# Two places of a two-block transformer kernel reordered: the first attention step of the second block inside the last values chunk, and the last gated chunk ahead of two down-projections

## The chip, the cores and the metric

The kernel runs on one NeuronCore of one Trainium2 chip. The metric is the device time of one execution in microseconds, the median of several runs; lower is better. Engines are named as the profile names them: PE (TensorE matmuls) and PEld (its weight loads), ACT (ScalarE), DVE (VectorE), POOL (GpSimd), SP (SyncE, which only issues DMAs here).

## The reference

256 tokens of width 1024 in fp32 pass through two blocks, each of depth 2. Only the parts that the change touches are shown.

```python
def swiglu_ffn(x, w_gu, w_down):                    # first block, FFN_HIDDEN 2816
    gu = x @ w_gu
    g, u = gu[..., :FFN_HIDDEN], gu[..., FFN_HIDDEN:]
    return (jax.nn.silu(g) * u) @ w_down

def conv_ffn(h, w_up, cw, cb, w_down):              # second block, D_FF 2816
    u = dwconv3(h @ w_up, cw) + cb
    g, val = jnp.split(u, 2, axis=-1)
    return (jax.nn.silu(g) * val) @ w_down

def diff_attention(q, k, v, lam):                   # second block, 8 heads
    s = jnp.einsum('bqahd,bkahd->bahqk', q, k).astype(jnp.float32) * (B_QK_DIM ** -0.5)
    p = jax.nn.softmax(s, axis=-1)
    a = (p[:, 0] - lam * p[:, 1]).astype(v.dtype)
    return jnp.einsum('bhqk,bkhe->bqhe', a, v)
```

The second block runs a full layer three times: once for the 256 context tokens (layer 0; keys and values of the context alone, "2 key tiles") and twice for the 256 latent tokens (layers 0 and 1; keys and values of latents and context, "4 key tiles"). Each of the three has one `diff_attention` and one `conv_ffn`.

## The kernel before

**Weights as a stream.** Every weight matrix is cut on the host into 908 units of 128 x 1024 fp32 (512 KB), in the order in which they are used. SP loads them into four slots `raw`. ACT converts a unit to the high part (`whi`, `hi_part`, L1017), POOL subtracts to get the low part (`wlo`, L448), and PE multiplies three times, high x high, high x low and low x high (L469 to L471 with features as the output's partitions, L495 to L497 with tokens). A unit of the usual kind is 24 matmuls of 256 columns, a unit of a token chunk 12 of 512 columns. `hi_part` for a unit waits until PE has finished the unit four places earlier (`units_used`), so ACT and POOL are at most four units ahead of PE, and everything that ACT does in between stands in the same queue as these conversions.

**The feed-forward.** `ffn_units` gives the order: 11 chunks `gate_up(j)` of four units and 11 `down_pair(j)` of two. Chunk 0 first, then for i = 0 to 4: gate_up(2i+1), down_pair(2i), gate_up(2i+2), down_pair(2i+1); the last pair, for chunk 10, is cut in halves (`last_blocks`). Between a chunk and its pair, `hidden` turns the chunk in PSUM `lin` into the operand of the pair. With the convolution (second block) that is: DVE 12 operations on 128 x 256 (L1827, L1830, L1834), ACT Silu (L1263), DVE product (a `tt_`, L1458), ACT copy to the high part `br_hi` (L1265), DVE subtraction to `br_lo` (L1458), which raises `hid_lo`, for which PE waits before the pair. ACT stands in `hidden` from the chunk's end until `br_hi` is written, and makes its next conversion only then. The operand tiles have two buffers, by the parity of the chunk. In the first block there is no convolution, and the chain is short.

**The second block's attention.** `second_layer` ends its projections with two token chunks (`token_chunk(0)`, `token_chunk(1)`: the values of heads 0 to 3 and 4 to 7). ACT copies each out of PSUM (L1034) and then raises `values_ready`. Then PE runs 16 steps n (8 heads x 2 query tiles): `diff_scores(n)` (L909), DVE `highest` (maximum of both halves L1992, then a small product with the query scale, L1458), ACT `diff_exps` (L1319, which first needs the Exp table), DVE `combine` (reciprocal L2001, small product L1458, L2004, L2006), PE `diff_transposes` (L916), ACT `transposed` (L1070), PE `diff_values` (L925). Units of the following gate and branch projections are put between them (`advance(fill, ...)`): one before the transposes, one or two before the values. Scores of n+1 are issued right after the transposes of n, those of n = 0 ahead of everything, after a wait for `qk_done` and `values_ready`. On ACT, the Exp of the two lambdas (L1376; it loads the Exp table) and `diff_exps(0)` stand behind the copy of the last values chunk; DVE waits for `lam_exp` before `highest(0)`. The order is written out by hand on every engine, and the engines meet only by semaphores.

Of the kernel before, what the change touches and what calls it, by code (L numbers as in the profile page):

```python
# [11 lines left out]
P, D, T, L = 128, 1024, 256, 2  # L12
KD = D // P
CH = 512
SLOTS, UNIT = 4, 1024
FFN = 2816
NCH = FFN // 256
# [50 lines left out]
def ffn_units(chunk, unit, gu, down):  # L68
    def gate_up(j):
        chunk(gu, j * CH)  # L70

    def down_pair(j):
        for k in (2 * j, 2 * j + 1):
            unit(down, [(k, 0)], D)

    gate_up(0)
    for i in range(NCH // 2):
        gate_up(2 * i + 1)
        down_pair(2 * i)
        gate_up(2 * i + 2)  # L80
        down_pair(2 * i + 1)
    for half in range(2):
        unit(down, [(2 * NCH - 2, half * CH), (2 * NCH - 1, half * CH)], CH)
# [127 lines left out]
def build(nc, a, n_units, n_first, n_dve):  # L211
    with ExitStack() as ctx:
# [238 lines left out]
        def _(pe):  # L451
# [121 lines left out]
            def ffn(after=(), context_norm=False):  # L573
# [13 lines left out]
                for b in range(4):  # L587
                    pe.matmul(aux[:, b, :].rearrange("p (n t) -> p n t", n=8),
                              zero_w[:, 0:1].to_broadcast([P, P]), zero_w[:, :].unsqueeze(1).to_broadcast([P, 8, 64]), start=True, stop=False, skip_group_check=True)
                for _ in range(NCH // 2):  # L590
                    feature_chunk(1)
                    down(0)
                    feature_chunk(0)
                    down(1)
                pe.wait_ge(hid_lo, t.next(hid_lo))
                for h in range(2):
                    last_blocks(aux_tile, 0, h, (br_hi, br_lo))

# [320 lines left out]
            def diff_values(n, kts):  # L919
                h, tt = divmod(n, 2)  # L920
                if tt == 0 and t.ahead(yb_taken, 0):
                    pe.wait_ge(yb_taken, t.ahead(yb_taken, 0))
                pe.wait_ge(pt_ready, t.next(pt_ready))
                for kt in range(kts):
                    mm = pe.matmul(aux[:, 3, tt * P:(tt + 1) * P], probs_tr[:, kt * P:(kt + 1) * P], head_values(h, kt, kts),  # L925
                                   start=(kt == 0), stop=(kt == kts - 1))
                mm.then_inc(pv_done, 1)
                if tt == 1:
                    t.skip(yb_taken)
# [19 lines left out]

            def second_layer(kts, rotate, start):  # L950
                start()
                token_chunk(1)
                feature_chunk(0, after={2: spatial_mix})
                for c in range(4):
# [5 lines left out]
                    else:  # L960
                        token_chunk(0, after=after)
                token_chunk(1)
                pe.wait_ge(qk_done, t.ahead(qk_done, 0))
                pe.wait_ge(values_ready, t.next(values_ready))
                fill = second_fill()
                diff_scores(0, kts)
                for n in range(STEPS):
# [33 lines left out]
            token_chunk(1, after={0: lambda: spread_inverse(0)})  # L1001
            second_layer(4, True, lambda: feature_chunk(0, fresh=QUARTERS))
            second_layer(4, True, normed_chunk)

        @block.scalar
        def _(act):
# [246 lines left out]
            def ffn(conv, context_norm=False):  # L1253
                def hidden(p, units):
                    hi_parts(units)
# [8 lines left out]
                    act.wait_ge(hid_f32, t.next(hid_f32))  # L1264
                    act.activation(br_hi[:, p * CH:(p + 1) * CH], zt(base + 12 + 2 * p, 2), ACT.Copy).then_inc(hid_hi, 1)  # L1265

                hidden(0, 4)
                for i in range(NCH // 2):
                    hidden(1, 4)
                    hidden(0, 6)  # L1270
                    if context_norm and i == NCH // 2 - 1:
                        for q in range(4):
                            quarter_hi(q, ctx_scaled[:, quarter(q)])
                    hi_parts(2)


# [68 lines left out]
            def second_layer(l, x, kts, rotate, normed=None):  # L1345
# [23 lines left out]
                values_chunk(0, zt(v, 4), qk_roots)  # L1369
                values_chunk(1, zt(v + 4, 4))  # L1370
                act.drain()
                if rotate and l == 1:
                    act.wait_ge(kv_landed, t.next(kv_landed, 32))
                act.drain().then_inc(values_ready, 1)
                act.wait_ge(lam_sum, t.next(lam_sum))
                act.activation(small[:, 18:20], small[:, 16:18], ACT.Exp).then_inc(lam_exp, 1)  # L1376
                fill = second_fill()
                diff_exps(0, kts)
                for n in range(STEPS):
# [69 lines left out]
        def _(dve):  # L1449
# [369 lines left out]
            def ffn(l, conv, context_norm=False):  # L1819
                def hidden(p, count, j):  # L1820
                    if conv:
# [26 lines left out]
                    else:  # L1848
                        settle().then_inc(lin_free[p], 1)
                    dve.wait_ge(hid_hi, t.next(hid_hi))  # L1850
                    tt_(br_lo[:, p * CH:(p + 1) * CH], h, br_hi[:, p * CH:(p + 1) * CH].bitcast(F32),
                        ALU.subtract).then_inc(hid_lo, 1)

                hidden(0, 4, 0)
                for i in range(NCH // 2):
                    hidden(1, 4, i * 2 + 1)
                    hidden(0, 6, i * 2 + 2)
                    lo_parts(2)
                    if context_norm and i < 4:
                        context_quarter(i)  # L1860
                if context_norm:
                    for q in range(4):
                        quarter_lo(q, ctx_scaled[:, quarter(q)])
# [407 lines left out]
```

## Time and profile before

| | |
|---|---|
| median of 3 runs | 3052.51 us (3045.93 to 3053.8) |
| the profiled execution | 3043.33 us |
| its span, first to last instruction | 3041.5 us |
| mean granted TensorE clock | 0.972 |
| PE, ACT, DVE, POOL busy | 96%, 50%, 36%, 72% |
| DMA | 495 MB, 163 GB/s |

The profile is of one execution, which was 9.2 us faster than the median of the three timed ones. A timeline row gives start, length, engine, line, operation, what it writes and reads, its shape, and in brackets the idle time of the engine before it and what ended it. "PEclk" is the clock that the throttle granted, 1.00 being 2.4 GHz and 0.50 being 1.2 GHz.

### The profile page before, as it was taken

Reading aid. Unit: us, or ns where it says so; the run is one execution under the profiler, and the core shown is the slowest. Engines: PE = TensorE matmul, PEld = TensorE weight load, DVE = VectorE, ACT = ScalarE, POOL = GpSimd, SP = SyncE. Lnnn points to the kernel's source line nnn. Section 1 sums busy time; section 2 is a strip of 40 time slices with the busy share of each in tenths; the row PEclk is TensorE's granted clock in tenths of the full one; section 3 lists DMA queues with packets and bytes.
Section 4 is the critical chain, followed back from the end, with each engine's and each line's share of the span. In section 5 each row is a group of like instructions: output and inputs, shape, how many; then the busy total and the mean of one; then the engine's idle time right before and its main releaser. Section 6 shows DMA issues by size and latency. Waiting matters only on the chain.

```text
span 3041.5 us, 51872 instructions
## 1 busy us (share of the span) xinstructions
PE 2924.7 (96%) x21822; PEld 2695.1 (89%) x21822; DVE 1080.1 (36%) x1976; ACT 1516.7 (50%) x1999; POOL 2177.2 (72%) x912
## 2 busy tenths in 40 slices
PE   7998989999999999999999999999999999899998
PEld 7887969989878879989899999878899989789998
DVE  2412412023214232221563433426624343464433
ACT  4666464455665454453564444445544444465443
POOL 6667687886667678886576886665576866557686
PEclk9999999999999989999999999999999999999999
DMA  6445455554445455554344554543354554334454
GB/s 219 140 152 179 148 191 176 182 196 164 152 151 183 164 176 180 186 196 148 132 152 153 179 177 151 189 133 118 126 173 146 187 175 154 124 125 160 152 177 150
DMA packets 136521, 495.39 MB, mean 163 GB/s; under 512 B 15072, under 2 KB 17760, under 8 KB 135136
## 3 DMA queue, kind: packets, MB, share of 16 engines
q1 hardware_dynamic: 131904, 480.53, 47.3%
q10 hardware_dynamic: 4384, 11.54, 1.1%
q8 instruction: 172, 2.82, 0.4%
q14 instruction: 61, 0.50, 0.1%
HBM read 488.86 MB, written 3.15 MB: 162 GB/s over the span
## 4 chain that ended last, share of the span: by engine, by line
PE 83%; ACT 5%; DVE 5%; DVEq 2%; POOL 2%; issue 1%; ACTq 1%; DMA 1%; SPq 0%
PE lin L469 18%; PE lin L470 17%; PE lin L471 17%; PE aux L469 4%; PE aux L471 4%; PE aux L470 4%; PE lin L495 2%; PE lin L496 2%; PE lin L497 2%; PE aux L562 2%; ACT whi L1017 2%; POOL wlo L448 2%; PE aux L909 1%; PE aux L633 1%; PE aux L925 1%
## 5 line engine op out<-in xcount | busy, mean ns | idle before, releaser
L448 POOL TENSOR_TENSOR wlo<-raw,whi 128x1024 fp32r<-128x1024 f32 x908 | 2177.0, 2414 | 850.0 <-ACT whi L1017 849.3
L1017 ACT ACTIVATE whi<-raw 128x1024 fp32r<-128x1024 f32 x908 | 949.7, 1057 | 990.3 <-PE lin L471 731.9
L469 PE MATMUL lin<-in_hi,whi 128*128 128x256 f32 x3968 | 1148.7, 289 | 24.7 <-POOL wlo L448 22.0
L470 PE MATMUL lin<-in_lo,whi 128*128 128x256 f32 x3968 | 1130.2, 285 | 0.0
L471 PE MATMUL lin<-in_hi,wlo 128*128 128x256 f32 x3968 | 1129.6, 285 | 0.0
L469 PEld LDWEIGHTS lin<-in_hi,whi 128*128 128x128 f32 x3968 | 769.2, 194 | 62.6 <-issue 52.7
L470 PEld LDWEIGHTS lin<-in_lo,whi 128*128 128x128 f32 x3968 | 769.6, 194 | 0.6
L471 PEld LDWEIGHTS lin<-in_hi,wlo 128*128 128x128 f32 x3968 | 768.7, 194 | 0.0
L469 PE MATMUL aux<-br_hi,whi 128*128 128x256 f32 x880 | 250.0, 284 | 7.6 <-DVE br_lo L1458 7.6
L471 PE MATMUL aux<-br_hi,wlo 128*128 128x256 f32 x880 | 249.8, 284 | 0.0
L470 PE MATMUL aux<-br_lo,whi 128*128 128x256 f32 x880 | 249.7, 284 | 0.0
L469 PE MATMUL lin<-br_hi,whi 128*128 128x256 f32 x768 | 224.6, 292 | 0.0
L470 PE MATMUL lin<-br_lo,whi 128*128 128x256 f32 x768 | 220.4, 287 | 0.0
L471 PE MATMUL lin<-br_hi,wlo 128*128 128x256 f32 x768 | 220.3, 287 | 0.0
L469 PEld LDWEIGHTS aux<-br_hi,whi 128*128 128x128 f32 x880 | 169.7, 193 | 8.2 <-DVE br_lo L1458 8.2
L471 PEld LDWEIGHTS aux<-br_hi,wlo 128*128 128x128 f32 x880 | 169.7, 193 | 0.0
L470 PEld LDWEIGHTS aux<-br_lo,whi 128*128 128x128 f32 x880 | 169.6, 193 | 0.0
L1827 DVE TENSOR_SCALAR Z<-lin,par_all 128x256 f32<-128x256 f32 x132 | 62.7, 537 | 272.7 <-PE lin L471 272.7
L469 PEld LDWEIGHTS lin<-br_hi,whi 128*128 128x128 f32 x768 | 150.5, 196 | 5.3 <-issue 3.5
L470 PEld LDWEIGHTS lin<-br_lo,whi 128*128 128x128 f32 x768 | 150.5, 196 | 0.2
L471 PEld LDWEIGHTS lin<-br_hi,wlo 128*128 128x128 f32 x768 | 150.5, 196 | 0.0
L1458 DVE TENSOR_TENSOR Z<-Z,lin 128x512 f32<-128x512 f32 (+1 forms) x34 | 29.8, 876 | 306.3 <-ACT Z L1263 277.1
(247 smaller groups left out, 3663.4 us busy)
## 6 DMA issues: line engine op xcount, KB each, us to landing
raw<-in_wstream SPq DMA_DIRECT2D x908, 512.0 KB, 3.3
Z<-in_rel ACTq DMA_DIRECT2D x2, 1536.0 KB, 7.3
Z<-in_mem_t ACTq DMA_DIRECT2D x2, 1024.0 KB, 7.4
kv_store<-Z ACTq DMA_DIRECT2D x2, 1024.0 KB, 6.9
Z<-kv_store ACTq DMA_DIRECT2D x2, 1024.0 KB, 10.8
x<-in_x_t SPq DMA_DIRECT2D x1, 1024.0 KB, 4.8
Z<-in_ctx_t SPq DMA_DIRECT2D x1, 1024.0 KB, 4.8
out_x<-x SPq DMA_DIRECT2D x1, 1024.0 KB, 3.8
```

What stands on the lines that cost most here:

```text
L448: pool.tensor_tensor(wlo[s][:, :], raw[s][:, :], whi[s][:, :].bitcast(F32), ALU.subtract).then_inc(lo_pool, 1)
L469: pe.matmul(out, wh, xh, start=start, stop=False, skip_group_check=True)
L470: pe.matmul(out, wh, xl, start=False, stop=False, skip_group_check=True)
L471: return pe.matmul(out, wl, xh, start=False, stop=stop, skip_group_check=True)
L495: pe.matmul(out, xh, wh, start=start, stop=False, skip_group_check=True)
L496: pe.matmul(out, xh, wl, start=False, stop=False, skip_group_check=True)
L497: return pe.matmul(out, xl, wh, start=False, stop=stop, skip_group_check=True)
L562: mm = pe.matmul(square_sums(b)[:, tt:tt + 1], zt(tiles + k)[:, tt * P:(tt + 1) * P], ones[:, 0:1], start=(k == 0 and tt == 0), stop=(k == ...
L633: mm = pe.matmul(out, q[:, tt * P:(tt + 1) * P], k[:, 0:(tt + 1) * P], start=True, stop=True)
L909: mm = pe.matmul(aux[:, m, 0:kts * P], q, head_keys(m, h, kts), start=True, stop=True)
L1017: act.activation(whi[s][:, :], raw[s][:, :], ACT.Copy).then_inc(hi_ready, 1)
L1827: dve.tensor_scalar(o[c], u[c], w[c][:, 1:2], w[c][:, 3:4], ALU.mult, ALU.add)
```

## The change

1. In each of the five feed-forwards, the last two chunks stand together: ... down_pair(7), gate_up(9), gate_up(10), down_pair(8), down_pair(9), and the halves for chunk 10. For that the operand tiles have three buffers (chunk modulo 3). ACT's conversions and, where it is there, its work on the context norm are divided anew over the end of the feed-forward. No unit is added or dropped.
2. In each of the three second layers, PE issues `diff_scores(0)` after the second of the four units of the last values chunk, behind a wait for `qk_done` and, in the last layer, for `kv_landed` (the loads of the stored context keys and values). `values_ready` is now waited for ahead of the first `diff_values`. On ACT the two-lambda Exp comes before the last values chunk's conversions, three conversions follow, then `diff_exps(0)`, then the fourth conversion and the copy. DVE and POOL keep their order.

```diff
@@ ffn_units
-    for i in range(NCH // 2):
+    for i in range(NCH // 2 - 1):
         gate_up(2 * i + 1)
         down_pair(2 * i)
         gate_up(2 * i + 2)
         down_pair(2 * i + 1)
+    for j in (NCH - 2, NCH - 1):
+        gate_up(j)
+    for j in (NCH - 3, NCH - 2):
+        down_pair(j)
@@ PE, ffn
-                for _ in range(NCH // 2):
+                for i in range(NCH // 2 - 1):
                     feature_chunk(1)
-                    down(0)
+                    down(2 * i % 3)
                     feature_chunk(0)
-                    down(1)
+                    down((2 * i + 1) % 3)
+                feature_chunk(1)
+                feature_chunk(0)
+                down((NCH - 3) % 3)
+                down((NCH - 2) % 3)
                 pe.wait_ge(hid_lo, t.next(hid_lo))
                 for h in range(2):
-                    last_blocks(aux_tile, 0, h, (br_hi, br_lo))
+                    last_blocks(aux_tile, (NCH - 1) % 3 * 2, h, (br_hi, br_lo))
@@ PE, diff_values
+                if n == 0:
+                    pe.wait_ge(values_ready, t.next(values_ready))
@@ PE, second_layer
+                def first_scores():
+                    pe.wait_ge(qk_done, t.ahead(qk_done, 0))
+                    if stored:
+                        pe.wait_ge(kv_landed, t.next(kv_landed, 32))
+                    diff_scores(0, kts)
...
-                token_chunk(1)
-                pe.wait_ge(qk_done, t.ahead(qk_done, 0))
-                pe.wait_ge(values_ready, t.next(values_ready))
+                token_chunk(1, after={1: first_scores})
                 fill = second_fill()
-                diff_scores(0, kts)
@@ ACT, ffn (DVE's hidden alike: buffer j % 3)
-                for i in range(NCH // 2):
-                    hidden(1, 4)
-                    hidden(0, 6)
-                    if context_norm and i == NCH // 2 - 1:
-                        for q in range(4):
-                            quarter_hi(q, ctx_scaled[:, quarter(q)])
+                for i in range(NCH // 2 - 1):
+                    hidden(2 * i + 1, 4)
+                    hidden(2 * i + 2, 6)
                     hi_parts(2)
+                hidden(NCH - 2, 4)
+                hidden(NCH - 1, 4)
+                for q in range(4):
+                    if context_norm:
+                        quarter_hi(q, ctx_scaled[:, quarter(q)])
+                    hi_part()
@@ ACT, second_layer
                 values_chunk(0, zt(v, 4), qk_roots)
-                values_chunk(1, zt(v + 4, 4))
+                act.wait_ge(lam_sum, t.next(lam_sum))
+                act.activation(small[:, 18:20], small[:, 16:18], ACT.Exp).then_inc(lam_exp, 1)
+                hi_parts(3)
+                diff_exps(0, kts)
+                evacuate(1, 1, zt(v + 4, 4))
                 act.drain()
                 if rotate and l == 1:
                     act.wait_ge(kv_landed, t.next(kv_landed, 32))
                 act.drain().then_inc(values_ready, 1)
-                act.wait_ge(lam_sum, t.next(lam_sum))
-                act.activation(small[:, 18:20], small[:, 16:18], ACT.Exp).then_inc(lam_exp, 1)
                 fill = second_fill()
-                diff_exps(0, kts)
```

## Rows read from the trace of the kernel before

**Rows 1.** The page's first part, busy time and share of the span by engine.

```profile
PE 2924.7 (96%) x21822; PEld 2695.1 (89%) x21822; DVE 1080.1 (36%) x1976; ACT 1516.7 (50%) x1999; POOL 2177.2 (72%) x912
```

**Rows 2.** PE's waits: us in total, how often, longest.

```profile
PE aux L916 <- DVE probs L2006: 19.1, 11, 3.2
PE aux L469 <- DVE br_lo L1458: 7.6, 3, 2.5
PE aux L909 <- ACTq L1374: 6.9, 3, 2.3
```

**Rows 3.** Timeline of PE at the three attention starts.

```profile
1452.64 0.44 PE L916 MATMUL aux<-c,probs 128*128 128x128 f32 x2 [0.32 <-DVE probs L2006]
...
2050.23 1.12 PE L916 MATMUL aux<-c,probs 128*128 128x128 f32 x4 [2.89 <-DVE probs L2006]
...
2607.07 1.13 PE L909 MATMUL aux<-Z 64*128 64x512 f32 x4 [2.30 <-ACTq L1374]
...
2614.47 0.66 PE L916 MATMUL aux<-c,probs 128*128 128x128 f32 x4 [3.22 <-DVE probs L2006]
```

**Rows 4.** Timeline of ACT at the third attention start.

```profile
2594.95 1.01 ACT L1034 ACTIVATE Z<-lin 128x1024 f32<-128x1024 f32 x1
...
2602.14 1.06 ACT L1017 ACTIVATE whi<-raw 128x1024 fp32r<-128x1024 f32 x1 [1.66 <-PE lin L497]
2604.86 1.06 ACT L1017 ACTIVATE whi<-raw 128x1024 fp32r<-128x1024 f32 x1 [1.66 <-PE lin L497]
...
2606.99 1.28 ACT L1376 ACT_TABLE_LOAD   x1 [0.15 <-issue]
...
2610.51 0.75 ACT L1319 ACTIVATE aux<-aux,small,qk_inv 128x512 f32<-128x512 f32 x1 [2.03 <-DVEq L1995]
```

**Rows 5.** Timeline of DVE at the same place.

```profile
2608.52 0.16 DVE L1458 TENSOR_TENSOR small<-small 128x1 f32<-128x1 f32 x1 [19.02 <-ACT small L1376]
...
2608.99 1.23 DVE L1992 TENSOR_REDUCE small<-aux 128x2 f32<-128x1024 f32 x1
...
2612.19 0.17 DVE L2001 RECIPROCAL small<-small 128x2 f32<-128x2 f32 x1 [1.74 <-ACTq L1320]
...
2613.67 0.75 DVE L2006 SCALAR_TENSOR_TENSOR probs<-aux,small,probs 128x512 f32<-128x512 f32 x1
```

**Rows 6.** A small DVE product beside POOL: timelines, and its group.

```profile
1461.33 2.40 POOL L448 TENSOR_TENSOR wlo<-raw,whi 128x1024 fp32r<-128x1024 f32 x1 [0.41 <-ACT whi L1017]
...
1461.76 1.98 DVE L1458 TENSOR_TENSOR small<-small,qk_inv 128x2 f32<-128x2 f32 x1
...
L1458 DVE TENSOR_TENSOR small<-small,qk_inv 128x2 f32<-128x2 f32 x48 | 38.0, 791 | 3.6
```

**Rows 7.** Timelines of PE, ACT and DVE at the second convolution feed-forward's end.

```profile
2472.45 0.39 PE L469 MATMUL aux<-br_hi,whi 128*128 128x256 f32 x1 [2.52 <-DVE br_lo L1458]
...
2469.66 0.63 ACT L1263 ACTIVATE Z<-Z 128x512 f32<-128x512 f32 x1 [4.32 <-DVEq L1837]
...
2471.58 1.99 ACT L1017 ACTIVATE whi<-raw 128x1024 fp32r<-128x1024 f32 x2
...
2470.32 0.69 DVE L1458 TENSOR_TENSOR Z<-Z 128x512 f32<-128x512 f32 x1 [0.74 <-ACT Z L1263]
...
2471.70 0.69 DVE L1458 TENSOR_TENSOR br_lo<-Z,br_hi 128x512 fp32r<-128x512 f32 x1 [0.69 <-ACT br_hi L1265]
```

**Rows 8.** Timeline of POOL over that feed-forward's last two chunks.

```profile
2455.43 9.50 POOL L448 TENSOR_TENSOR wlo<-raw,whi 128x1024 fp32r<-128x1024 f32 x4 [3.06 <-ACT whi L1017]
...
2462.52 7.13 POOL L448 TENSOR_TENSOR wlo<-raw,whi 128x1024 fp32r<-128x1024 f32 x3
```

**Rows 9.** Stretches: length, busy (instructions) of PE, PEld, DVE, ACT, POOL, PEclk, DMA.

```profile
1447.00:1455.00 8.00, 7.61 (x45) 6.53 (x46) 3.54 (x10) 4.00 (x8) 2.82 (x2) 0.79 0.33 126
2047.00:2059.00 12.00, 9.11 (x48) 7.08 (x48) 4.86 (x10) 5.57 (x11) 2.35 (x1) 0.72 0.13 47
...
2860.00:3020.00 160.00, 160.00 (x1336) 160.00 (x1335) 60.74 (x128) 69.18 (x77) 130.10 (x55) 1.00 0.54 180
```

More of the change, by code:

```diff
@@ L948, in branch_transposes, with second_layer @@
                         mm.then_inc(yb_trans, 1)
-            def second_layer(kts, rotate, start):
+            def second_layer(kts, rotate, start, stored=False):
+                def first_scores():
[3 more added lines that the diff above has]
+                    diff_scores(0, kts)
                 start()
@@ L1001, in _ @@
             token_chunk(1, after={0: lambda: spread_inverse(0)})
-            second_layer(4, True, lambda: feature_chunk(0, fresh=QUARTERS))
-            second_layer(4, True, normed_chunk)
+            for l in range(L):
+                second_layer(4, True, normed_chunk if l else lambda: feature_chunk(0, fresh=QUARTERS), l == 1)
         @block.scalar
@@ L1253, in ffn, with hidden @@
             def ffn(conv, context_norm=False):
-                def hidden(p, units):
+                def hidden(j, units):
+                    p, b = j % 2, j % 3
                     hi_parts(units)
@@ L1264, in hidden @@
                     act.wait_ge(hid_f32, t.next(hid_f32))
-                    act.activation(br_hi[:, p * CH:(p + 1) * CH], zt(base + 12 + 2 * p, 2), ACT.Copy).then_inc(hid_hi, 1)
+                    act.activation(br_hi[:, b * CH:(b + 1) * CH], zt(base + 12 + 2 * p, 2), ACT.Copy).then_inc(hid_hi, 1)
                 hidden(0, 4)
-                for i in range(NCH // 2):
-                    hidden(1, 4)
-                    hidden(0, 6)
-                    if context_norm and i == NCH // 2 - 1:
-                        for q in range(4):
-                            quarter_hi(q, ctx_scaled[:, quarter(q)])
-                    hi_parts(2)
+                for i in range(NCH // 2 - 1):
+                    hidden(2 * i + 1, 4)
+                    hidden(2 * i + 2, 6)
+                    hi_parts(2)
+                hidden(NCH - 2, 4)
[4 more added lines that the diff above has]
+                    hi_part()
             def rms(x, fresh=False, then=None):
@@ L1819, in ffn, with hidden @@
             def ffn(l, conv, context_norm=False):
-                def hidden(p, count, j):
+                def hidden(j, count):
+                    p, b = j % 2, j % 3
                     if conv:
@@ L1850, in hidden @@
                     dve.wait_ge(hid_hi, t.next(hid_hi))
-                    tt_(br_lo[:, p * CH:(p + 1) * CH], h, br_hi[:, p * CH:(p + 1) * CH].bitcast(F32),
+                    tt_(br_lo[:, b * CH:(b + 1) * CH], h, br_hi[:, b * CH:(b + 1) * CH].bitcast(F32),
                         ALU.subtract).then_inc(hid_lo, 1)
[L1854 to L1857, printed above, removed]
+                hidden(0, 4)
+                for i in range(NCH // 2 - 1):
+                    hidden(2 * i + 1, 4)
+                    hidden(2 * i + 2, 6)
                     lo_parts(2)
-                    if context_norm and i < 4:
+                    if context_norm:
                         context_quarter(i)
+                hidden(NCH - 2, 4)
+                hidden(NCH - 1, 4)
+                lo_parts(4)
                 if context_norm:
```

## Prediction

> **What bounds the kernel now.** First the page's busy times: PE works 96% of the span, POOL 72% [rows 1]. Then a stretch in the middle of a feed-forward: 1336 matmuls in 160 us without a pause, at full clock [rows 9]. That is 0.120 us each, so a unit of 24 matmuls takes 2.87 us, two 5.75, four 11.5. No reordering makes that shorter. A change of order can win only where PE stands still, and what the clock loses there. So the third view is the list of PE's waits [rows 2]. Three of its groups lie where the diff moves something: DVE's `br_lo` before a feed-forward's last halves (7.6 us, 3 times, always in the convolution form), ACT at L1374, which is `values_ready`, before the first scores (6.9 us, 3 times), and DVE's `probs` before transposes (19.1 us, 11 times). Of these 11, three are the first step of an attention, 0.32, 2.89 and 3.22 us [rows 3], in sum 6.43; the other eight (12.7 us) belong to later steps, which the change leaves as they are. The two feed-forwards without convolution wait nowhere at that point, so reordering them gives nothing.
>
> **Part 1, the feed-forward's end.** Count from G, the end of the last gate-up chunk. In the second convolution feed-forward PE's wait ends at 2472.45 after 2.52 us [rows 7], and two units stand before it, so G = 2472.45 - 2.52 - 5.75 = 2464.18. The chain that starts there has Silu at G+5.5, DVE's product at G+6.1, ACT's next conversions at G+7.4 and `br_lo` ready at G+8.2 [rows 7]. It needs 8.2 us and has two units of cover. After the change four units stand there, 11.5 us, a margin of 3.3. Chunk 9 has chunk 10 and pair 8 as cover, 17.2 us. The gap goes three times: 7.6 us.
>
> What is late next? ACT makes no conversion while it is in that chain, and now two chains follow each other after four units, not six. After chunk 9 the first conversion starts at G9+7.4, and POOL's product from 8.5 to 11.0 (in the trace 2455.43, G9 being 2446.9 [rows 8]). PE wants that unit at 11.5: margin 0.5, the same as in every turn of the old loop. POOL then has four units back to back, 9.50 us [rows 8], until G9+18.05, which is G10+6.5. DVE's product of chunk 10 reads two SBUF tiles and starts at G10+6.1. Such a product waits for POOL: a 128 x 2 one took 1.98 us and ended with POOL's instruction of 1461.33 to 1463.73 [rows 6]. So it loses at most 0.4 us, the conversion starts by G10+7.8, POOL is done at 7.8+1.06+0.08+2.40 = 11.35, and PE wants the unit at 11.5. I take 0; the bounds are 0 and a whole POOL instruction less the margin, 2.4-0.5 = 1.9 each, 5.7 in all. The third buffer costs no instruction. The halves' units come in the same number and size, and SP's queue only sees another order.
>
> **Part 2, the first attention step.** Take the third start and count from A, the end of the second unit of the last values chunk. The scores now start at 2607.07 after a wait of 2.30, so the chunk ends at 2604.77 [rows 3]. Conversions released by its units start 2.72 apart [rows 4], so a unit is 2.72 and A = 2599.33. After the change:
> - PE: scores 0 to 1.1 (1.13 [rows 3]), third unit to 3.8, fourth to 6.5, then the first fill unit. That takes 3.05 (from 2608.20, the scores' end, to 2611.25, where the wait of 3.22 begins [rows 3]), until 9.55. Then PE wants the transposes.
> - ACT: the first values copy ends at A-3.4 [rows 4]; table load 1.28 and the Exp follow, to about -1.75, beside PE's first two units. The first conversion starts at -1.7 instead of -2.6 and has 8 us in hand. The second starts at 0.1. The third waits for the third unit: 3.9 to 4.95. Only then come the exponentials, 1.68 us (2610.51 to DVE's reciprocal at 2612.19 [rows 4, 5]), to 6.6. The fourth conversion waits for the end of the fourth unit (6.5) anyway and loses 0.1. So does the values copy behind it, which ends near 8.7; the new wait for `values_ready` stands before `diff_values(0)` at about 14.3 (9.55, transposes 0.66, scores 1.13, a unit 3.05) and costs nothing.
> - DVE: it now stood idle 19.02 us for the lambda Exp [rows 5]; afterwards that is long done. Maximum from 1.2 to 2.45. The small product meets POOL, whose instruction for the second conversion runs until about 4.25, and waits for it, but the exponentials start at 4.95 in any case. After them the reciprocal at 6.65, then a small product that meets POOL's third instruction (5.0 to 7.4), then L2004 and L2006, some 1.7 of the 2.23 us from reciprocal to the end of L2006 [rows 5]: probabilities at 9.1 to 9.3 against 9.55.
>
> Both waits go: 6.9 + 6.43 = 13.3 us. The first start has 2 key tiles, shorter operations and more margin. `kv_landed` in the last layer is for loads that ACT issues at the layer's start, ten chunks earlier, and costs 0; if late it would have held `values_ready` too. What is late next is the second small product: if it misses the gap between two POOL instructions it waits to 10.1, probabilities come at 11.8, and PE waits 2.2 us, in two starts 4.4. That is the bound.
>
> This meeting is where a rule of the Trainium skill speaks against the change: SBUF — State Buffer, "Who interferes with whom", calls the port pair of VectorE and GpSimd an exclusive lock, so that a VectorE instruction with two SBUF inputs is blocked for the whole of a GpSimd one. The trace agrees (1.98 us for two columns [rows 6]). By that rule alone the old place had a merit, POOL being idle there; by the times above the lock is mostly covered.
>
> **The clock.** Around two of the three attention starts the granted clock was low, 0.79 over 8 us and 0.72 over 12 us [rows 9]; a third stretch, 8 us around the wait of 2472.45 [rows 7], repeats the row with 0.79. At half clock PE loses 8 x 0.21 + 12 x 0.28 + 8 x 0.21 = 6.7 us, some 0.7 of it while it waited. All three follow a wait that goes; the other three places had such waits at full clock. I take 6.0, with 0 and 10 (all six places) as bounds. TensorE: Matmul & The Clock Gate, "What's actually happening", says that the monitor's window runs free and that a kernel's slow matmuls differ in number from run to run; no run here shows it for one place.
>
> **The sum.** 7.6 + 13.3 + 6.0 = 26.9 us. Against the profiled execution's 3043.3 that is 3016.4. But that execution was 9.2 us below the median of the timed runs, 3052.5, and I forecast a median: 3052.5 - 26.9 = **3025.6, say 3026**.
>
> **Rivals.**
> - *The clock part doesn't come*, because slow stretches fall elsewhere. For it: three of six such waits had none. Gain 20.9: 3031.6. Chance 0.15.
> - *POOL's lock gives half of it back*: 2.2 us in two starts and 1.9 us at three feed-forwards' ends, 10.1 in all. For it: margins of 0.2 to 0.5 us. Against it: every term is from rows of the same code at other places. 3035.7; with the slow clock back after the new waits 3041.7. Chance 0.12. The Trainium skill's lock rule, named above, gives this case if the lock falls badly every time.
> - *The scores don't start the chain earlier* (part 2 does not do what it says), since ACT's queue order, not PE, holds the probabilities. Against it: the exponentials end at 6.6 by the rows. Only part 1 with its clock share is left, 7.6 + 1.7: 3043.2. Chance 0.06.
> - *Slower*: the earlier first step shifts DVE against POOL in all 48 steps, so that each small product with `qk_inv` waits a whole POOL instruction, 2.40, and not the mean of 0.79 [rows 6]. That adds 1.61 to each step's chain, 77 us if nothing covers it: 3103. It decides from 0.56 us a step (26.9 / 48). For it: eight later steps already wait for `probs`, so the cover is thin. Against it: each step starts anew at its transposes, and the order inside the loop is the same. Chance 0.05.
>
> **How the numbers follow.** The forecast has 0.62, with a range of its own of 3015 to 3035 (clock part 0 to 10, some microseconds between sessions). With the first two rivals it makes 0.89; a range of 3013 to 3041 leaves out the last two and the tails. A measurement of this kernel can tell about 0.3%, 9 us, from no change. Faster by more, below 3043.4: 0.62 + 0.15 + 0.12 less tails, 0.87. Within: 0.08, of which the third rival is most. Slower: 0.05.
>
> **What would show it.** In the profile after, L909's first scores stand between L495 to L497 matmuls with no idle time before them; the first L916 of each attention has no idle time of 0.3 us or more; `br_lo` no longer appears among PE's waits with 2.5 us, and no `wlo` wait stands before the last halves. The eight later waits stay near 12.7 us in sum. I am wrong if new `wlo` waits appear at the feed-forwards' ends, if the first L916 waits 2 us, or if the later `probs` waits grow.

## The result and the profile after

The changed kernel takes 3018.61 us (median of 4 runs) against 3051.14 us for the kernel before, measured on the same chip; the ratio is 0.9899, 95% interval 0.9882 to 0.9917, which is 25 to 36 us less. A second measurement gave 3023.53 against 3046.28, ratio 0.9921 (0.9901 to 0.9941), 18 to 30 us less. The forecast was 3026, that is 26.9 us less than the 3052.5 it started from.

The page's first part of the changed kernel, and three rows of PE's waits (us in total, how often, longest):

```profile
PE 2919.8 (97%) x21822; PEld 2692.0 (89%) x21822; DVE 1097.9 (36%) x1976; ACT 1515.8 (50%) x1999; POOL 2179.8 (72%) x912
...
PE aux L924 <- DVE probs L2028: 12.6, 8, 2.9
PE aux L566 <- ACT Z L1301: 4.8, 5, 3.5
PE aux L473 <- POOL wlo L452: 1.8, 2, 0.9
```

Of the three groups of [rows 2], `probs` has gone from 19.1 us in 11 waits to 12.6 in 8. `br_lo` before the last halves and `values_ready` before the first scores appear no more, and no `wlo` wait has taken their place (1.8 us in 2 waits, as before). The second row has grown: the token sums of a norm wait 4.8 us for ACT's squares, where they waited 3.4 (L562 in the kernel before).

The third attention start, to be laid beside [rows 3 to 5]. PE (matmul rows of the scores and the transposes), ACT, DVE, then POOL:

```profile
2583.52 1.13 PE L917 MATMUL aux<-Z 64*128 64x512 f32 x4
...
2593.05 0.49 PE L924 MATMUL aux<-c,probs 128*128 128x128 f32 x3
...
2580.24 1.28 ACT L1388 ACT_TABLE_LOAD   x1
...
2587.71 1.06 ACT L1030 ACTIVATE whi<-raw 128x1024 fp32r<-128x1024 f32 x1 [2.96 <-PE lin L501]
2588.68 0.73 ACT L1336 ACTIVATE aux<-aux,small,qk_inv 128x512 f32<-128x512 f32 x1
...
2584.70 1.23 DVE L2014 TENSOR_REDUCE small<-aux 128x2 f32<-128x1024 f32 x1 [2.53 <-PE aux L917]
2586.00 1.53 DVE L1476 TENSOR_TENSOR small<-small,qk_inv 128x2 f32<-128x2 f32 x1
2590.34 0.17 DVE L2023 RECIPROCAL small<-small 128x2 f32<-128x2 f32 x1 [2.81 <-ACTq L1337]
2590.58 0.68 DVE L1476 TENSOR_TENSOR small<-small 128x1 f32<-128x1 f32 x1
...
2592.00 0.75 DVE L2028 SCALAR_TENSOR_TENSOR probs<-aux,small,probs 128x512 f32<-128x512 f32 x1
...
2582.77 4.75 POOL L452 TENSOR_TENSOR wlo<-raw,whi 128x1024 fp32r<-128x1024 f32 x2 [0.98 <-ACT whi L1030]
2588.85 2.40 POOL L452 TENSOR_TENSOR wlo<-raw,whi 128x1024 fp32r<-128x1024 f32 x1 [1.33 <-ACT whi L1030]
```

Neither PE row has idle time in brackets: both waits are gone. With A = 2583.52 the probabilities are ready at 2592.75, A+9.2, and PE turns to the transposes at A+9.5. Both small products end with a POOL instruction: the first takes 1.53 us until 2587.53 (POOL's pair ends at 2587.52), the second 0.68 until 2591.26 (POOL ends at 2591.25).

The end of the second convolution feed-forward, against [rows 7 and 8], and the start of the last layer behind it. The first two rows are the kernel before at that start (ACT's last conversion ahead of the norm, and PE's token sums), all others the changed kernel:

```profile
2477.17 1.06 ACT L1017 ACTIVATE whi<-raw 128x1024 fp32r<-128x1024 f32 x1 [3.60 <-PE aux L471]
2482.20 1.15 PE L562 MATMUL aux<-c,Z 128*128 128x1 f32 x8 [2.25 <-ACT Z L1284]
...
2452.03 2.94 ACT L1030 ACTIVATE whi<-raw 128x1024 fp32r<-128x1024 f32 x3
...
2450.55 0.91 DVE L1476 TENSOR_TENSOR Z<-Z 128x512 f32<-128x512 f32 x1 [0.75 <-ACT Z L1277]
2452.16 0.69 DVE L1476 TENSOR_TENSOR br_lo<-Z,br_hi 128x512 fp32r<-128x512 f32 x1 [0.70 <-ACT br_hi L1279]
...
2453.15 11.81 POOL L452 TENSOR_TENSOR wlo<-raw,whi 128x1024 fp32r<-128x1024 f32 x5 [2.24 <-ACT whi L1030]
...
2455.59 0.33 SPq L441 DMA_DIRECT2D raw<-in_wstream  x1
...
2460.11 1.06 ACT L1030 ACTIVATE whi<-raw 128x1024 fp32r<-128x1024 f32 x1 [3.03 <-DMA raw<-in_wstream]
2460.12 0.34 ACTq L1363 DMA_DIRECT2D Z<-in_sgu_w  x1
...
2463.17 1.28 ACT L1295 ACT_TABLE_LOAD   x1 [2.00 <-issue]
...
2462.73 2.27 DVE L1473 TENSOR_SCALAR mod<-mods_all 128x48 f32<-128x48 f32 x1
...
2455.76 0.30 PE L473 MATMUL aux<-br_hi,whi 128*128 128x256 f32 x1
2465.15 0.37 PE L566 MATMUL aux<-c,Z 128*128 128x1 f32 x1 [3.45 <-ACT Z L1301]
```

`br_lo` is ready at 2452.85, 2.9 us before PE starts the last halves at 2455.76. POOL, which ACT's chain held idle for 2.24 us, then runs five instructions back to back until 2464.96, past the end of the feed-forward (2461.70, where PE's wait of 3.45 us begins). A slot of the weight stream comes free only when POOL has read it, so SP issues the transfer of the unit that ACT converts at 2460.11 only at 2455.59, when the first of the five is done, and ACT waits 3.03 us for it to land. ACT's load issues, its table load and the first square (2464.47) follow in its queue, and PE's token sums wait 3.45 us, where they waited 2.25.

**A way to count.** In every kernel of this study PE's time can be split into three parts. I take the second part of the execution, from the wait of 0.52 us in the token sums near 1330 us to PE's last product. Ahead of it the change takes no wait away (PE's idle time there is 65.5 and 69.3 us in the two executions of before, 65.6 and 65.9 in the two of the changed kernel), yet over all traces it began between 1323.0 and 1331.8 us. Within the second part I add up PE's idle times over 0.3 us, and half of the time at granted clock 0.50. What is left is called PE's own work (where PE waited at half clock, half of that time is counted twice, and the rest comes out smaller by it):

| kernel | second part | idle | clock | rest | timed ratio to before (95%) |
|---|---|---|---|---|---|
| before | 1708.1 | 43.0 | 37.5 | 1627.6 | |
| before_again | 1703.9 | 42.2 | 34.1 | 1627.6 | |
| after | 1681.9 | 24.1 | 30.7 | 1627.1 | 0.9899 (0.9882 to 0.9917) |
| after_again | 1683.0 | 24.1 | 32.4 | 1626.5 | 0.9921 (0.9901 to 0.9941) |
| attn_only | 1690.9 | 29.6 | 34.1 | 1627.2 | 0.9932 (0.9911 to 0.9953) |
| ffn_only | 1696.3 | 35.7 | 32.4 | 1628.2 | 0.9961 (0.9944 to 0.9977) |
| busy_before | 1703.6 | 24.7 | 30.7 | 1648.2 | 0.9984 (0.9970 to 0.9998) |
| scores_u3 | 1684.0 | 25.9 | 30.7 | 1627.4 | 0.9905 (0.9875 to 0.9934) |
| double_small | 1683.7 | 26.5 | 27.3 | 1629.9 | 0.9925 (0.9896 to 0.9953) |
| late_loads | 1682.1 | 22.6 | 30.7 | 1628.8 | 0.9918 (0.9898 to 0.9938) |
| square_psum | 1673.1 | 16.7 | 29.0 | 1627.4 | 0.9877 (0.9857 to 0.9898) |
| both_fix | 1674.6 | 18.6 | 27.3 | 1628.7 | 0.9884 (0.9866 to 0.9902) |
| all_fix | 1668.5 | 18.6 | 22.2 | 1627.7 | 0.9876 (0.9858 to 0.9895) |
| before_square | 1691.3 | 34.7 | 27.3 | 1629.3 | 0.9952 (0.9933 to 0.9970) |

The rest agrees within 3.4 us over all kernels but the one that adds products. So the means of two executions each say where the gain is: 23.6 us (1706.0 to 1682.4), of which 18.5 is idle time (42.6 to 24.1) and 4.2 clock (35.8 to 31.6). The clock alone moves by 1.7 and 3.4 us between the two executions of one kernel, as much as the 4.2 us, so the clock's share of the gain isn't secured by this table. Over the whole span the two executions of each differ by 22.0 us (3041.5 and 3040.0 against 3017.7 and 3019.8).

### The profile page after: what moved, and what is told of

Read it like the earlier page. It is cut to its first block, busy times and chain, and to the rows that moved or that the text cites. A ratio compares the mean times of both kernels' runs of the same rounds, so it can differ in the third digit from the quotient of the medians.

```text
span 3017.7 us, 51871 instructions
## 1 busy us (share of the span) xinstructions
PE 2919.8 (97%) x21822; PEld 2692.0 (89%) x21822; DVE 1097.9 (36%) x1976; ACT 1515.8 (50%) x1999; POOL 2179.8 (72%) x912
## 4 chain that ended last, share of the span: by engine, by line
PE 83%; ACT 5%; DVE 4%; POOL 2%; DVEq 2%; issue 1%; ACTq 1%; DMA 1%; SPq 0%
PE lin L473 18%; PE lin L474 17%; PE lin L475 17%; PE aux L473 4%; PE aux L475 4%; PE aux L474 4%; POOL wlo L452 2%; PE lin L499 2%; PE aux L566 2%; PE lin L501 2%; PE lin L500 2%; ACT whi L1030 2%; PE aux L641 1%; PE aux L917 1%; PE lin L616 1%
## 6 DMA issues: line engine op xcount, KB each, us to landing
Z<-kv_store ACTq DMA_DIRECT2D x2, 1024.0 KB, 12.7
```

## The experiments

### The two halves of the change

attn_only is the kernel before with the attention hunks of the diff, ffn_only the one with the feed-forward hunks; after_again is the changed kernel once more, on the same chip.

> The changed kernel once more, on the chip on which its two halves are timed. By the sum of the prediction, 7.6 + 13.3 us of waits and about 6 us of clock, it stands 27 us under the kernel before; the first measurement had 25 to 36 us. Theory A: what the two parts gain alone adds up to this gain, to within 3 us. Theory B: the gain has a third source, over 26.9 us, that comes only with both; then the sum of the parts falls short by 5 us or more.

> Only the first attention step is moved; the feed-forwards are those of before. Theory A: the three waits before the first scores (6.9 us) and the three before the first transposes (6.4 us) go, with 0 to 5 us of clock: 13 to 18 us faster than before, some 3035. PE still waits 2.52 us three times for br_lo. Rival, POOL's lock catches the second small product: 4.4 us of that come back as probs waits, 9 to 14 us faster.

> Only the feed-forward's order and its third buffer; the attention's start is that of before. Theory A: three waits of 2.52 us go, 7.6 us, with 0 to 3 us of clock, less about 1.4 us at the last block's start, where in the changed kernel the token sums waited 3.45 us and not 2.25: 6 to 9 us faster, some 3043. Rival, the two chains close together hold POOL up and PE waits for wlo before the last halves: 0 to 4 us faster, with new wlo waits of 1 us or more.

Measured: 0.9932 is 21 us less (14 to 27) for the attention, 0.9961 is 12 us less (7 to 17) for the feed-forward. By the second part they are 15.1 and 9.7 us, in sum 24.8, against 23.6 with both. The parts add up to within 1.2 us, and theory A holds; a third source would have left 5 us. PE's idle time says the same: 13.0 us less for the attention (13.3 forecast), 6.9 for the feed-forward (7.6 forecast). The timed medians can't decide it: their parts make 33 us against 24 with both, with intervals of 5 to 7 us to each side of every figure. The waits split cleanly. PE's waits in attn_only, then in ffn_only:

```profile
PE aux L916 <- DVE probs L2012: 12.6, 8, 2.9
PE aux L469 <- DVE br_lo L1464: 7.6, 3, 2.5
...
PE aux L924 <- DVE probs L2022: 19.3, 11, 2.9
PE aux L917 <- ACTq L1386: 6.9, 3, 2.3
PE aux L566 <- ACT Z L1296: 3.1, 5, 2.0
```

attn_only keeps the three `br_lo` waits and has lost the first-step ones; ffn_only is the reverse. The wait of the token sums, which I had put down to the reorder with 1.4 us, was 2.0 us in ffn_only, no longer than before. The traces of all kernels show why. Let E be the end of the second feed-forward. ACT's last conversion before the sums can start at E-2.78, when PE frees its slot. In the old order its transfer was issued at E-11.2 to E-12.7 and had 8 us and more to land. In the new order it is issued at E-6.1 in all nine traces, which leaves 3.3 us. In two of them (ffn_only, double_small) it landed within that, in the other seven it took 4.3 to 5.0 us, and the conversion came 0.9 to 1.7 us late. So it is the reorder that takes the room away, and the transfer's time in the execution at hand that decides whether the conversion is late. A second part of the wait doesn't depend on it: from this conversion to the table load ACT's five load issues took 2.5 to 3.2 us, but 3.75 in double_small, which waited 2.96 us though its transfer had landed in time.

### The clock alone

```diff
                 pe.wait_ge(qk_done, t.ahead(qk_done, 0))
+                keep_busy(10)
                 pe.wait_ge(values_ready, t.next(values_ready))
...
                     advance(fill, DIFF_BEFORE_T[n])
+                    if n == 0 and kts == 4:
+                        keep_busy(12, 3)
                     diff_transposes(n, kts)
...
+                if second:
+                    pe.wait_ge(lin_free[1], t.ahead(lin_free[1]))
+                    for _ in range(11):
+                        pe.matmul(lin[:, 1, 0:CH]...)
                 pe.wait_ge(hid_lo, t.next(hid_lo))
```

> The kernel before with its order untouched; PE fills most of the waits that the change removes with products nobody reads: 10 before the wait for values_ready (three places), 12 before the first transposes (the two starts with four key tiles), 11 before the wait for br_lo (three places), about 0.21 us each at full clock. The output is that of before. No wait is shortened, so this shows the clock's share alone. Theory A, the half-clock stretches around these places follow from PE's standing still: 3 to 8 us faster than before, and the three stretches at the third and fourth of these places gone. Theory B, they fall where they fall: no difference, or up to 3 us slower where a product runs past the end of its wait.

> The kernel before once more, for where its half-clock stretches fall. Theory A, they follow the waits: of the nine waits that the change removes (2.3 to 3.2 us each, one of 0.3 to 1.8) again some three are followed by such a stretch within 8 us, and the second part's clock loss is 34 to 38 us. Theory B, chance: they fall at other places, and as often where PE does not wait.

Measured: 0.9984, 5 us less, with the interval from 1 to 9; by the second part 2.4 us less than the mean of the two executions of before, with 5.1 us less clock loss and 2 to 3 us lost where a product ran past the end of its wait or a wait was not quite filled. The timed gain lies in theory A's range of 3 to 8 us, the trace's 2.4 us just under it. The granted clock (last but two columns: PEclk) around such a wait, in attn_only and in ffn_only where it stays, and in busy_before where the waits of 2035 to 2055 and of 2455 to 2470 are filled:

```profile
2458.00:2470.00 12.00, 9.48 (x67) 9.28 (x66) 6.36 (x14) 4.22 (x5) 8.44 (x5) 0.86 0.53 172
...
2590.00:2606.00 16.00, 11.79 (x64) 8.41 (x63) 4.91 (x10) 8.01 (x12) 7.78 (x4) 0.89 0.40 129
...
2035.00:2055.00 20.00, 19.61 (x125) 14.23 (x124) 6.56 (x14) 10.03 (x16) 9.71 (x5) 1.00 0.35 112
2455.00:2470.00 15.00, 14.87 (x115) 13.28 (x115) 9.22 (x20) 5.28 (x6) 11.96 (x6) 1.00 0.57 181
```

Counting places over all traces says more. The change touches six places (three attention starts, three feed-forward ends). In the executions that still wait 2.3 us or more there (before, before_again, before_square, and the kept half of attn_only and ffn_only) these are 24 places, and in 14 of them PE's clock fell to half from about the wait's end; which ones differed between two executions of the same kernel (3 of 6 each time, two of them the same). Where the wait is gone or filled there are 60 places, and in none did it fall (one of these, the first attention start of busy_before, still waited 1.9 us). So the fall follows PE's standing still, and which of the waits is hit changes from one execution to the next, as theory A of before_again had it (its clock loss, 34.1 us, lies in the forecast range). The half-clock stretches at the six places cost 6.8 us in before, 5.1 in before_again and 6.8 in before_square. In the total this hardly shows, since the stretches at other places differ as much: before_square, which has these waits, lost 27.3 us, less than either trace of the changed kernel (30.7 and 32.4). The Trainium skill, TensorE: Matmul & The Clock Gate, "What's actually happening", says the monitor runs free of the kernel; the traces agree, with 14 of 24.

### How much room the first step has

```diff
-                token_chunk(1, after={1: first_scores})
+                token_chunk(1, after={2: first_scores})
```

> The changed kernel with the first scores one unit (2.72 us) later, behind the third unit of the last values chunk and not the second. By the prediction's chain: maximum A+3.9 to 5.2, the small product waits for POOL's instruction of A+5.0 to 7.4, exponentials to 9.3, probabilities at A+11.9 against a need at 9.55. Theory A: PE waits about 2.4 us for probs in the two starts with four key tiles and 0.5 to 1.5 in the first, 5 to 6 us slower than the changed kernel in all. Theory B, the chain has more room than worked out: no such waits, no difference.

Measured: the second part is 1.6 us longer than the changed kernel's mean; `probs` waits come back at the two starts with four key tiles, but of 0.45 and 0.78 us, not 2.4. That is neither theory A (5 to 6 us slower) nor B (no waits). PE, DVE and POOL at the third start:

```profile
2589.65 0.55 PE L924 MATMUL aux<-c,probs 128*128 128x128 f32 x3 [0.78 <-DVE probs L2028]
...
2584.39 1.24 DVE L1476 TENSOR_TENSOR small<-small,qk_inv 128x2 f32<-128x2 f32 x1
...
2587.61 0.16 DVE L1476 TENSOR_TENSOR small<-small 128x1 f32<-128x1 f32 x1
...
2578.44 7.17 POOL L452 TENSOR_TENSOR wlo<-raw,whi 128x1024 fp32r<-128x1024 f32 x3 [0.97 <-ACT whi L1030]
2588.61 2.36 POOL L452 TENSOR_TENSOR wlo<-raw,whi 128x1024 fp32r<-128x1024 f32 x1 [3.00 <-ACT whi L1030]
```

The scores come 2.72 us later and the probabilities only some 1.1 us later against PE's need (0.3 us ahead of it before, 0.78 behind now). My sum let POOL's instructions stand where they were. But POOL works on what ACT converts, and ACT's exponentials now stand ahead of the fourth conversion: POOL runs dry for 3.00 us, and just then the second small product finds it idle and takes 0.16 us. The chain that is late makes room for itself. The placement in the change has 0.3 us to spare (A+9.2 against A+9.5); one unit later it misses by 0.45 and 0.78 us.

### The slower rival

```diff
+                    tt_(small[:, 224:226], stat(n, "minus"), query_scale(n), ALU.mult)
+                    settle()
                     tt_(stat(n, "minus"), stat(n, "minus"), query_scale(n), ALU.mult)
```

> The changed kernel with the small product with qk_inv (128 x 2, two SBUF inputs, 0.16 us when free, mean 0.79) done twice in each of the 48 steps, the first time into scratch. It prices the rival in which DVE and POOL meet badly in every step. Theory A, the steps' chains are covered but for the eight that already wait: 0.3 to 2.4 us in each of these, 2 to 19 us slower than the changed kernel. Theory B, nothing covers the steps: 48 times 0.8 us and more, 38 us slower or worse.

Measured: 0.9925, and a second part 1.3 us longer than the changed kernel's mean. PE's waits for `probs`, which were 12.6 us in 8 waits:

```profile
PE aux L924 <- DVE probs L2030: 15.4, 10, 3.4
```

2.8 us more in sum. The clock loss is 4.3 us smaller than the changed kernel's mean in this execution; without it the second part is 5.5 us longer, 2.4 of them idle. Theory A (2 to 19 us), near its lower end: the steps have cover, also against a product that meets POOL, and the waits that exist grow by 0.2 to 0.8 us. The first product of a pair takes the wait for POOL, the second is then free (median of all 96 is 0.163 us).

### What makes the later steps wait

The eight waits that the change leaves are the largest thing left in the attention. Before one of them, DVE's square of a head's output stands in the queue ahead of the next maximum. DVE and POOL of the changed kernel before the wait of 2.87 us at 2637.72:

```profile
2630.34 0.41 DVE L2034 TENSOR_SCALAR probs<-aux 128x256 f32<-128x256 f32 x1
2630.88 2.43 DVE L2036 SCALAR_TENSOR_TENSOR probs<-probs 128x256 f32<-128x256 f32 x1
...
2630.63 2.39 POOL L452 TENSOR_TENSOR wlo<-raw,whi 128x1024 fp32r<-128x1024 f32 x1 [0.53 <-ACT whi L1030]
```

The square has both inputs in SBUF and ends 0.3 us after POOL's instruction; the clamp ahead of it reads PSUM and takes its 0.41 us beside the same POOL instruction. So the square is given one input from PSUM, at the price of one more clamp, of the head's output in PSUM:

```diff
                     dve.tensor_scalar(sq, y, 2.0 ** 64, -2.0 ** 64, ALU.min, ALU.max)
-                    settle().then_inc(yb_taken, 1)
-                    dve.scalar_tensor_tensor(sq, sq, 2.0 ** -10, sq, ALU.mult, ALU.mult)
+                    dve.tensor_scalar(y, y, 2.0 ** 64, -2.0 ** 64, ALU.min, ALU.max)
                     settle()
+                    dve.scalar_tensor_tensor(sq, y, 2.0 ** -10, sq, ALU.mult, ALU.mult)
+                    settle().then_inc(yb_taken, 1)
```

> The changed kernel, where DVE's squares of the head outputs (24, one for every two steps, two SBUF inputs, 0.42 us when free, median 1.84, up to 2.6) take one input from PSUM, at the price of one more clamp of 0.42 us each. The output stays. Theory A, the eight waits for probs in later steps (12.6 us) come from this square waiting for POOL: they fall to about 4 us (2.9 to 1.4, 2.6 to 1.1, the short ones to 0), 8 to 11 us faster than the changed kernel. Theory B, ACT's or PE's order sets them: the squares get short and the waits stay.

> The kernel before, with nothing but the squares of the head outputs taking one input from PSUM. Theory A, the eight later waits for probs come from the squares in the old order too: the group falls from 19.1 us to about 12 (the three first steps, 6.4, and 5.2), some 9 us faster than before; the waits that the change removes stay. Theory B, without the change's earlier first step the waits of later steps are set otherwise and stay near 12.7 us.

Measured: square_psum is at 0.9877 of before, its second part 9.3 us shorter than the changed kernel's. The groups of the squares (count | busy, mean ns) in the changed kernel and in square_psum, the waits for `probs` in square_psum and in before_square:

```profile
L2036 DVE SCALAR_TENSOR_TENSOR probs<-probs 128x256 f32<-128x256 f32 x24 | 37.4, 1557 | 3.0
...
L2037 DVE SCALAR_TENSOR_TENSOR probs<-aux,probs 128x256 f32<-128x256 f32 x24 | 10.2, 424 | 2.0
...
PE aux L924 <- DVE probs L2028: 5.2, 6, 1.2
...
PE aux L916 <- DVE probs L2006: 9.9, 9, 2.9
PE aux L469 <- DVE br_lo L1458: 7.6, 3, 2.5
PE aux L909 <- ACTq L1374: 6.9, 3, 2.3
```

24 squares go from 1557 to 424 ns. The waits fall by 7.4 us after the change, and by 9.2 us in the old order (19.1 to 9.9, where about 12 was expected; one first step waits 1.4 us there and not 2.9, behind a stretch at half clock). before_square's second part is 14.7 us shorter than before's mean where some 9 us was forecast; 7.9 of them are idle time, and 8.5 are clock, which its edit can't be credited with from one execution. Theory A in both: the three waits of 2.6 to 2.9 us shrink to 1.0 to 1.2, the two of 1.2 go, and only the two of 0.8 us stay as they were and have another cause.

### The start of the last layer

late_loads moves ACT's five load issues of the last layer behind the token norm; both_fix adds the edit of square_psum; all_fix also loads the norm's table ahead of the feed-forward's last conversion.

```diff
+                if normed is not None:
+                    rms(x, normed, ACT.Gelu_apprx_tanh)
                 act.dma_start(zt(S2, 2), a["sgu_w"]...)
...
-                if normed is not None:
-                    rms(x, normed, ACT.Gelu_apprx_tanh)
```

> The changed kernel, with ACT's five loads at the last block's start issued behind the token norm and not ahead of it (in the other two blocks that start without a norm nothing changes). In the changed kernel the token sums there waited 3.45 and 3.8 us for ACT's square, behind a conversion whose transfer landed late (2460.11), 3.0 us of issues and a table load of 1.28. Theory A, the issues stand on the path: the wait is 1.2 to 1.8 us, some 2 us faster than the changed kernel, 26 to 30 us faster than before by the sum of waits. Theory B, the late transfer alone sets it: the wait stays at 3 us or more and the time is that of the changed kernel.

> The changed kernel with the squares of the head outputs taking one input from PSUM and with ACT's loads behind the token norm. Theory A, the two are independent: 9.4 us (second part of square_psum against that of the changed kernel, by its trace) and 0 to 2 us for the loads, 9 to 11 us faster than the changed kernel, 33 to 36 us faster than before. Theory B, with the waits for probs gone POOL and ACT fall differently and the loads' gain turns negative: not faster than square_psum by its trace.

> both_fix, and ACT loads the table for the token norm ahead of the feed-forward's last conversion, where it stands idle for 2 to 3 us, and not behind it. Theory A, the table load of 1.28 us stands on the path to the token sums: the wait there falls from 1.5 to 0.3 us, those of 0.4 to 0.5 us at the other start go, 1.5 us faster than both_fix by the trace. Theory B, the residual or the late transfer holds the sums: the wait stays above 1 us.

Measured: in late_loads the wait falls to 1.49 us, as theory A said, but the idle time in all falls by 1.5 us only, since new waits appear, and the second part is no shorter (1682.1 against 1682.4), the rest being 2.1 us larger, which is inside the scatter of 3.4 us. Two new waits of PE in late_loads, the same two in both_fix, and what DVE did in both_fix:

```profile
2489.57 0.47 PE L499 MATMUL lin<-whi,in_hi 128*128 128x512 f32 x1 [0.70 <-POOL wlo L452]
2509.96 1.27 PE L909 MATMUL aux<-Z 128*128 128x128 f32 x9 [0.59 <-DVE Z L2076]
...
2477.73 0.47 PE L499 MATMUL lin<-whi,in_hi 128*128 128x512 f32 x1 [0.91 <-POOL wlo L452]
2500.03 1.16 PE L909 MATMUL aux<-Z 128*128 128x128 f32 x8 [2.54 <-DVE Z L2077]
...
2477.46 0.29 DVE L1476 TENSOR_TENSOR probs<-Z 128x128 f32<-128x128 f32 x1 [5.21 <-DMA Z<-in_lam]
2477.67 2.35 DVE L1476 TENSOR_TENSOR small<-par_all,c 128x1 f32<-128x1 f32 x1
...
2494.78 5.20 DVE L2077 TENSOR_SCALAR Z<-Z,small 128x512 f32<-128x512 f32 x2
```

The issues take their 3 us of ACT's queue wherever they stand: now they hold up the conversions behind the norm, and DVE waits 5.21 us for the lambdas to land. DVE's two `TENSOR_SCALAR` then fall beside POOL and take 5.20 us, where the changed kernel's took 1.33 at the same place. In late_loads theory A was right on the wait, and its 2 us of gain don't show; in both_fix theory B holds, 1.9 us more idle time than square_psum and a second part 1.5 us longer. all_fix cuts the wait to 0.56 us, but at the other start a wait of 2.04 us appears for DVE (1850.87), and its idle time is that of both_fix, 18.6 us. Its shorter second part is clock (22.2 against 27.3 us), which one execution can't credit to the edit. all_fix (3009.49, ratio 0.9876) and square_psum (3011.69, 0.9877) can't be told apart; both are faster than the changed kernel by their ratios to before (0.9899 and 0.9921) and by the trace.

## Why the prediction was right

- **What bounds the kernel, and the gap sum.** 6.9 + 6.43 + 7.6 = 20.9 us of waits were to go, and all nine went. PE's idle time fell by 18.5 us only. The missing 2.4 us are waits that grew elsewhere: 1.5 us in the mean are the token sums at the last layer's start (2.25 and 2.09 before, 3.45 and 3.83 after), 0.4 the same sums one layer earlier, the rest smaller ones.
- **Part 1.** Right in each number that could be read: chunk 10's product lost 0.22 us to POOL (0.91 instead of 0.69; at most 0.4 forecast), POOL stood idle 2.24 us and was done with the halves' unit 0.2 us before PE wanted it (0.15 forecast). The failed step is "The halves' units come in the same number and size, and SP's queue only sees another order". The number is the same, but they reach POOL in one block of five instructions, a slot comes free later, and the transfer behind it has 3.3 us to land, not 8 or more. I followed POOL to the last halves and not to the end of the stream that it feeds.
- **Part 2.** First conversion, exponentials, maximum, both meetings with POOL and the probabilities at A+9.2 came within 0.35 us of the forecast. The bound of 2.2 us a start, POOL's lock falling badly, was too dark: the runs give 0.5 us for the second small product, and scores_u3 shows why it can't fall much worse, since POOL runs dry when ACT is in the exponentials.
- **The clock.** Forecast 6.0 with 0 and 10 as bounds; 4.2 by two pairs of traces, and filling the waits alone gave 5 us (1 to 9) timed and 5.1 us less clock loss. Both traced figures are differences of a size that one kernel's executions show among themselves; that 6.0 was so near is in part luck. At the places themselves before lost 6.8 and 5.1 us in its two executions. The reason given, that slow stretches follow these waits and not others, is what 14 of 24 against 0 of 60 shows. That "all three follow a wait that goes" was right, but which three was chance, and part of it came back: in both traces of the changed kernel a stretch of 13.7 us at half clock stands at the longer wait of the token sums, where it was 10.2 us in both of before.
- **The rivals.** Clock part absent: excluded by busy_before only just (interval 1 to 9 us), by the count of places clearly. POOL's lock gives 10.1 us back: not so, no `wlo` or first-step `probs` wait is there. Scores don't start the chain earlier: excluded by attn_only. Slower through the steps' phase: the eight later waits are unchanged to 0.1 us, and a second small product in every step costs 1.3 us, or 5.5 with the clock left out, not 77 or 38.
- **The base.** I took the median of the runs and not the profiled execution as the base. The medians of before in four sessions were 3043.6 to 3051.1 us. The measured 3018.6 lies 7.4 us under the forecast, of which 1.4 are the base and the rest is a larger gain; the 3023.5 lies 2 us under it because a base 6.2 us lower and a smaller gain nearly cancel. The gain, 26.9 forecast, was 30.8 (of the ratio 0.9899) and 24.1 us timed, and 23.6 by the traces of the second part. That 26.9 lies between these is partly luck: the waits gave 2.4 us less than their term, and the clock's term can't be read to better than some 3 us.

## What to carry to other kernels

Where the bounding engine has a few waits of 2 to 3 us, find the chain behind each and count how many units of other work can stand in front of it; here two units more in one place and half a chunk in another took 20.9 us of waits, and each is a subtraction of rows. Then follow every queue past the place, not only to it: the engine that is now busy without a pause frees its buffers later, and the next stage pays. An issue or a load that is moved off the path costs its time again where it lands, if its queue is full there.

## What the runs showed of the hardware

- **DVE beside POOL.** A DVE instruction that reads one PSUM input keeps its time beside POOL (clamp 0.414 to 0.417 us over 24 of them); one with two SBUF inputs waits until POOL's instruction ends (square 0.425 to 2.60 us). That was known from [rows 6]. New was that it lengthens five of the eight later waits by 1.2 to 1.7 us, and that instructions with a single SBUF tensor as input and an SBUF output are held as well: the copy of `mod` (a `TENSOR_SCALAR` of 128 x 48) took 2.27 us beside POOL's instruction, ending with it at 2465.0, and 0.19 us without one in the kernel before, and the `TENSOR_SCALAR` of 128 x 512, which also reads a scalar of each partition, took 0.54 to 2.71 us. The Trainium skill, SBUF — State Buffer, "Who interferes with whom", names `tensor_scalar` among those that can enter a two-port mode and then contend with GpSimd; the traces agree in that it is held (2.27 against 0.19 us), and don't show its mode.
- **The granted clock** fell to half at 14 of 24 waits of 2.3 us and more, and at none of 60 places where the same wait was absent or filled with products. In the same kernel the places differ from one execution to the next; its loss in the second part differed by 3.4 us between the two executions of before and by 1.7 between those of the changed kernel. Over all the traces the loss in the first part, where no edit takes a wait away, was 37.5 to 51.2 us.
